# Gated delta rule: state steps that multiply keys by the state and send the residual through the inverse

## The reference, cut to what matters

```python
u = jnp.einsum('bhnij,bhnjv->bhniv', t_inv, v * beta)
w = jnp.einsum('bhnij,bhnjk->bhnik', t_inv, k_beta * jnp.exp(g)[..., None])
intra = jnp.einsum('bhnik,bhnjk->bhnij', q, k) * decay
q_dec = q * jnp.exp(g)[..., None]
k_dec = k * jnp.exp(g_last[..., None] - g)[..., None]

def step(state, inp):
    u_n, w_n, q_n, intra_n, k_n, dec_n = inp
    v_new = u_n - jnp.einsum('bhck,bhkv->bhcv', w_n, state)
    o_n = jnp.einsum('bhck,bhkv->bhcv', q_n, state) + jnp.einsum('bhcs,bhsv->bhcv', intra_n, v_new)
    state = state * dec_n[..., None, None] + jnp.einsum('bhck,bhcv->bhkv', k_n, v_new)
    return state, o_n
```

## Time and profile before

| what | value |
|---|---|
| runs | 1976.20, 1977.56, 1979.18 us |
| profiled execution, span | 1977.9 us |
| PE busy | 1908.4 us, 96% |
| DVE busy | 1473.9 us, 75% |
| ACT busy | 982.2 us, 50% |
| POOL busy | 314.5 us, 16% |
| mean DMA rate | 202 GB/s |
| chain that ended last | PE 70%, DVE 13%, DMA 6%, ACT 5%, issue 5% |
| eight heads | about 500 to 1134 us from the span's start |

### The profile page before, as it was taken

The page is one execution under the profiler, slowest core; times in us unless marked ns, Lnnn a source line. Parts: engine busy times, 40 slices in busy tenths (PEclk is TensorE's granted clock), DMA queues, the critical chain, the costliest instruction groups (busy, mean ns, idle before and its releaser), DMA issues.

```text
span 1977.9 us, 28478 instructions
## 1 busy us (share of the span) xinstructions
PE 1908.4 (96%) x9519; PEld 1584.6 (80%) x9519; DVE 1473.9 (75%) x1966; ACT 982.2 (50%) x1354; POOL 314.5 (16%) x243
## 2 busy tenths in 40 slices
PE   5999999999999999999999899998999999999996
PEld 5778888778888888888888787876888888888883
DVE  6966676676756858658577455677999999999996
ACT  5343223301453544535535343125888788788863
POOL 0332323001102101021011000001222222222210
PEclk7999999999999999999999999998999999999998
DMA  8133223687132222222232678437999999999966
GB/s 301 32 82 103 68 80 106 213 294 248 40 106 72 70 75 77 80 70 71 84 93 59 206 266 262 140 143 280 372 383 383 382 380 381 386 387 383 400 252 257
DMA packets 225500, 398.93 MB, mean 202 GB/s; under 512 B 50805, under 2 KB 163878, under 8 KB 199974
## 3 DMA queue, kind: packets, MB, share of 16 engines
q1 hardware_dynamic: 205254, 342.28, 49.8%
q10 hardware_dynamic: 10976, 39.15, 5.1%
q0 software_dynamic: 9216, 16.80, 2.2%
HBM read 356.89 MB, written 58.06 MB: 210 GB/s over the span
## 4 chain that ended last, share of the span: by engine, by line
PE 70%; DVE 13%; DMA 6%; ACT 5%; issue 5%; SPq 1%; ACTq 0%; DVEq 0%; POOL 0%; POOLq 0%
PE ps L3152 17%; PE ps L2756 13%; PE ps L769 12%; PE ps L3196 9%; PE ps L3047 4%; PE ps L2786 3%; PE ps L3138 1%; DVE vv L2019 1%; DMA inv_rows<-inv_d 1%; DMA so_lo<-o_lo_d 1%; DMA inv_d<-sub_x 1%; PE ps L2950 1%; PE ps L2980 1%; PE ps L3176 1%; PE ps L2994 1%
## 5 line engine op out<-in xcount | busy, mean ns | idle before, releaser
L637 DVE TENSOR_TENSOR mw_lo<-mw_raw,mw_hi 128x2048 fp32r<-128x2048 f32 x192 | 436.9, 2290 | 44.0 <-ACT mw_hi L632 43.8
L632 ACT ACTIVATE mw_hi<-mw_raw 128x2048 fp32r<-128x2048 f32 x192 | 368.1, 1919 | 116.2 <-PE ps L3152 67.0
L769 PE MATMUL ps<-h_hi,w_lo 128*128 128x512 f32 x704 | 287.9, 409 | 3.0 <-ACT mod_rows L1447 1.3
L769 PE MATMUL ps<-h_hi,w_hi 128*128 128x512 f32 x704 | 275.5, 391 | 0.0
L769 PE MATMUL ps<-h_lo,w_hi 128*128 128x512 f32 x704 | 274.9, 391 | 0.0
L3152 PE MATMUL ps<-mw_hi,xT_lo 128*128 128x512 f32 x512 | 203.9, 398 | 3.1 <-DVE xT_lo L2525 2.3
L3152 PE MATMUL ps<-mw_hi,xT_hi 128*128 128x512 f32 x512 | 201.1, 393 | 0.0
L3152 PE MATMUL ps<-mw_lo,xT_hi 128*128 128x512 f32 x512 | 200.3, 391 | 0.0
L769 PEld LDWEIGHTS ps<-h_hi,w_hi 128*128 128x128 f32 x704 | 132.6, 188 | 28.4
L769 PEld LDWEIGHTS ps<-h_hi,w_lo 128*128 128x128 f32 x704 | 133.0, 189 | 26.6 <-ACT conv_in L1454 1.8
L769 PEld LDWEIGHTS ps<-h_lo,w_hi 128*128 128x128 f32 x704 | 133.2, 189 | 22.3
(11 more groups left out here) (436 smaller groups left out, 4042.4 us busy)
## 6 DMA issues: line engine op xcount, KB each, us to landing
mw_raw<-in_w_dram SPq DMA_DIRECT2D x192, 1024.0 KB, 8.2
w_raw<-in_w_in_dram SPq DMA_DIRECT2D x44, 512.0 KB, 5.0
ada_h<-in_w_ada_dram SPq DMA_DIRECT2D x32, 512.0 KB, 6.0
pair_w<-in_w_in_dram SPq DMA_DIRECT2D x28, 512.0 KB, 4.8
y_t<-y_d SPq DMA_DIRECT2D x7, 1024.0 KB, 10.1
ada_sc<-in_w_ada_dram SPq DMA_DIRECT2D x4, 1024.0 KB, 8.7
s_d<-sc_acc ACTq DMA_DIRECT2D x8, 512.0 KB, 5.5
gate_b_d<-gate_sig ACTq DMA_DIRECT2D x8, 512.0 KB, 5.0
```

What stands on the lines that cost most here:

```text
L632: act.activation(mw_hi[off % NSPLIT][:], mw_raw[off % NRAW][:], ACT.Copy).then_inc(mw_hi_done, 1)
L637: dve.tensor_tensor(mw_lo[off % NSPLIT][:], mw_raw[off % NRAW][:], mw_hi[off % NSPLIT][:], ALU.subtract).then_inc(mw_lo_done, 1)
L769: last = pe.matmul(dst, lhs[:, s, k], rhs[:, k, cols], start=(k == 0 and part == 0), stop=(k == KD - 1 and part == 2))
```

## The change

The product of `k_bg` with `Y` and its copy `w_neg` are gone, and so are the `k_bg` copies. (The squares that used `k_bg` as a place to write go to a tile `square_out`.) The scale of the keys, now with the sign turned, is applied by a new DVE instruction in each step from t = 1: it multiplies the product of keys and state by the scale and adds it to `v_beta` in place (`r_done`). Only then does PE multiply `Y` by `v_beta`. So a step has three places where PE waits (`s_ready`, `r_done`, `vn_done`) and not two, and the six projection products of a step are dealt out two to each. On DVE the convolution's tap moves ahead of the state update.

```diff
@@ the projection helper
-                for part in range(3):
+                for part in parts:
@@ ACT, start of a head
-                act.wait_ge(k_root, 6 * h + 6)
-                act.wait_ge(k_dec_done, TT * h + TT)
-                for t in range(TT):
-                    act.activation(k_bg[:, t], ..., ACT.Copy, scale=hk[:, K_BG, t:t + 1]).then_inc(k_bg_done, 1)
@@ ACT, ahead of the state loop
-                for n in range(2):
-                    act.wait_ge(w_mm, past(2 * h + n + 1))
-                    act.activation(w_neg[:, 4 * n:4 * n + 4]..., ps[:, 6 + n], ACT.Copy,
-                                   scale=-1.0).then_inc(w_neg_done, 1)
@@ DVE, the state loop
+                dve.wait_ge(v_beta_done, TT * h + TT)
                 for t in range(TT):
+                    if t > 0:
+                        dve.wait_ge(ks_mm, (TT - 1) * h + t)
+                        dve.scalar_tensor_tensor(out=v_beta[:, t], in0=ps[:, 6 + t % 2, 0:P],
+                                                 scalar=hk[:, K_BG, t:t + 1], in1=v_beta[:, t],
+                                                 op0=ALU.mult, op1=ALU.add).then_inc(r_done, 1)
+                    if t >= 4 and not last:
+                        if t == 4:
+                            dve.wait_ge(bank_free, 2 + 2 * head_tile(h, 3) + 1)
+                        conv_tap(h + 1, 1, 1, qk[:, 1], 0, k_conv, t - 4)
                     if t < TT - 1:
                         dve.wait_ge(ds_mm, (TT - 1) * h + t + 1)
...
-                    if t >= 4 and not last:
-                        if t == 4:
-                            dve.wait_ge(bank_free, 2 + 2 * head_tile(h, 3) + 1)
-                        conv_tap(h + 1, 1, 1, qk[:, 1], 0, k_conv, t - 4)
@@ PE
-                for a in range(2):
-                    pe.wait_ge(y_upd, 2 * NL * h + 2 * (NL - 1) + a + 1)
-                    for t in range(4 * a, 4 * a + 4):
-                        last_mm = pe.matmul(ps[:, 6 + a, ...], k_bg[:, t], Y[:, t], start=True, stop=True)
-                    last_mm.then_inc(w_mm, 1)
...
                 for t in range(TT):
-                    if t % 4 == 0:
-                        pe.wait_ge(w_neg_done, 2 * h + t // 4 + 1)
+                    if t == 0:
+                        pe.wait_ge(y_upd, 2 * NL * h + 2 * NL)
+                    tok = slice(t * P, (t + 1) * P)
                     o_t = ps[:, 3 + t % 2, 0:P]
-                    last_mm = pe.matmul(ps[:, 2, 0:P], Y[:, t], v_beta[:, t], start=True, stop=(t == 0))
                     if t > 0:
                         pe.wait_ge(s_ready, (TT - 1) * h + t)
-                        last_mm = pe.matmul(ps[:, 2, 0:P], w_neg[:, t], S[:], start=False, stop=True)
-                    last_mm.then_inc(vn_mm, 1)
-                    if t >= 2:
-                        pe.wait_ge(o_copied, past(TT * h + t - 1))
-                    if t > 0:
+                        pe.matmul(ps[:, 6 + t % 2, 0:P], qk[:, 1, tok], S[:], start=True, stop=True).then_inc(ks_mm, 1)
+                        if t >= 2:
+                            pe.wait_ge(o_copied, past(TT * h + t - 1))
                         pe.matmul(o_t, S[:], q_dec[:, t], start=True, stop=False)
-                    filler(2 * t)
+                        filler(6 * t, 6 * t + 2)
+                        pe.wait_ge(r_done, (TT - 1) * h + t)
+                    pe.matmul(ps[:, 2, 0:P], Y[:, t], v_beta[:, t], start=True, stop=True).then_inc(vn_mm, 1)
+                    filler(6 * t + 2 if t else 0, 6 * t + 4)
                     pe.wait_ge(vn_done, TT * h + t + 1)
                     if t < TT - 1:
                         pe.matmul(ps[:, 5, 0:P], k_dec[:, t], v_new[:, t % 2], start=True, stop=True)\
                           .then_inc(ds_mm, 1)
                     pe.matmul(o_t, v_new[:, t % 2], intra[:, t], start=(t == 0), stop=True).then_inc(o_mm, 1)
-                    filler(2 * t + 1)
+                    filler(6 * t + 4, 6 * t + 6)
```

More of the change, by code:

```diff
@@ L260, in decoder_block @@
     intra = at("intra", [P, TT, P])
-    k_bg = at("k_bg", [P, TT, P])
+    square_out = at("square_out", [P, TT, P])
     k_dec = at("k_dec", [P, TT, P])
@@ L295, in decoder_block @@
     assert top[0] <= SCRATCH + 2 * 4 * TT * P
-    top[0] = SCRATCH + 4 * TT * P
-    w_neg = at("w_neg", [P, TT, P])
+    top[0] = SCRATCH + 2 * 4 * TT * P
     o_raw = at("o_raw", [P, T])
@@ L510, in decoder_block @@
         vt_mm = sem("vt_mm")
-        k_bg_done = sem("k_bg_done")
         k_dec_done = sem("k_dec_done")
@@ L521, in decoder_block @@
         y_upd = sem("y_upd")
-        w_mm = sem("w_mm")
-        w_neg_done = sem("w_neg_done")
+        ks_mm = sem("ks_mm")
+        r_done = sem("r_done")
         s_ready = sem("s_ready")
@@ L603, in decoder_block @@
                  q_dec_done, head_out, logits_done, h_hi_done, h_lo_done, mb_out, o_copied, x1_turned,
-                 sc_copied, gb_sig, root_done, x1T_done, w_mm, *m_out, *h2_out]
+                 sc_copied, gb_sig, root_done, x1T_done, *m_out, *h2_out]
         SHIFT_PARTS = KD + 1
@@ L1475, in key_norms @@
                         act.wait_ge(kt_mm, 2 * h + t // 4 + 1)
-                    ins = act.activation(k_bg[:, t], ps[:, 4 + t // 4, (t % 4) * P:(t % 4 + 1) * P], ACT.Square,
+                    ins = act.activation(square_out[:, t], ps[:, 4 + t // 4, (t % 4) * P:(t % 4 + 1) * P], ACT.Square,
                                          accum_out=k_stat[:, 0, t:t + 1])
@@ L1523, in head_act @@
                 evac_conv("head", h, 0, 0, 1)
-                act.wait_ge(k_root, 6 * h + 6)
-                act.wait_ge(k_dec_done, TT * h + TT)
-                for t in range(TT):
-                    act.activation(k_bg[:, t], ps[:, 4 + t // 4, (t % 4) * P:(t % 4 + 1) * P], ACT.Copy,
-                                   scale=hk[:, K_BG, t:t + 1]).then_inc(k_bg_done, 1)
                 evac_conv("head", h, 0, 1, 1)
@@ L1550, in head_act @@
                                    scale=hk[:, K_V, t:t + 1]).then_inc(v_beta_done, 1)
-                for n in range(2):
-                    act.wait_ge(w_mm, past(2 * h + n + 1))
-                    act.activation(w_neg[:, 4 * n:4 * n + 4].rearrange("p t i -> p (t i)"), ps[:, 6 + n], ACT.Copy,
-                                   scale=-1.0).then_inc(w_neg_done, 1)
                 for t in range(TT):
@@ L1950, in _ @@
             dve.wait_ge(gate_exp, 5)
-            dve.tensor_tensor(gates[:, G_KBG], grow_of[:].rearrange("p h t -> p t h"), gates[:, G_BETA], ALU.mult).then_inc(gate_step, 1)
+            dve.tensor_tensor(gates[:, G_KBG], grow_of[:].rearrange("p h t -> p t h"), gates[:, G_NBETA], ALU.mult).then_inc(gate_step, 1)
             dve.wait_ge(gate_step, 9)
@@ L2933, in head_pe @@
                             pe.wait_ge(kk_done, 4 * h + 4)
-                            pe.wait_ge(k_bg_done, TT * h + TT)
                             pe.wait_ge(k_dec_done, TT * h + TT)
@@ L2945, in head_pe @@
                             last_mm.then_inc(yl_mm, 1)
-                for a in range(2):
-                    pe.wait_ge(y_upd, 2 * NL * h + 2 * (NL - 1) + a + 1)
-                    for t in range(4 * a, 4 * a + 4):
-                        last_mm = pe.matmul(ps[:, 6 + a, (t % 4) * P:(t % 4 + 1) * P], k_bg[:, t], Y[:, t],
-                                            start=True, stop=True)
-                    last_mm.then_inc(w_mm, 1)
                 pe.wait_ge(q_dec_done, past(h + 1))
@@ L2958, in head_pe, with filler @@
                     bank_clear(pe, head_tile(H - 1, 3), 1)
[L2960 to L2974, removed]
+                def filler(first, end):
+                    width = H - 1 if last else KD
+                    for n in range(first, min(end, 2 * 3 * width)):
+                        half, k, part = n // (3 * width), n // 3 % width, n % 3
+                        if last and half == 0 and part == 0:
+                            pe.wait_ge(o_in[k // 4], (128, 96)[k // 4])
+                        if not last and k == 0 and part == 0:
+                            wait_w(pe, "head", h, 3)
+                            bank_clear(pe, head_tile(h, 3), half)
+                        phase, hi, lo = ("merge", so_hi, so_lo) if last else ("head", h_hi, h_lo)
+                        last_mm = project(pe, ps[:, half], phase, 0 if last else 3, hi, lo, half, ks=(k,), parts=(part,))
+                        if not last and k == KD - 1 and part == 2:
+                            last_mm.then_inc(proj_done, 1)
```

## The result

The changed kernel takes 1991.18 us (median of five runs, 1987.90 to 1992.79), the kernel before 1977.56 us (median of five) beside it. The medians differ by 13.6 us; the ratio is 1.0065, 95% interval 1.0053 to 1.0076, which is 12.9 us (10.5 to 15.0). Forecast were 1993.9 us and +16.3. The profiled execution has a span of 1989.2 us, 11.3 above that of before.

What follows compares the result with a forecast made beforehand. The heads' state loop was taken as bound by PE's own stream plus uncovered waits. Terms -8.0 + 11.6 + 10.6 + 2.1 = +16.3 us on the 1977.6 us median gave 1993.9 us; range 1985.5 to 2002.

Steps and rivals of the forecast that it cites:

- The bound: State loop of the heads: bound by PE's own stream; a wait costs only what projection products ahead do not cover.
- Start of the loop: Heads 0 to 6, before step 0: w_neg's products and wait go, v_beta late next; gain 1.14 us a head, 8.0 for seven.
- Steps: Heads 0 to 6, each loop step: three partly uncovered waits, 2.50 to 2.74 us; 1.65 us a head, 11.6 for seven.
- The restart of 0.16 us: PE at a wait nothing covers: load 0.05 us after the operand, product counted as started 0.11 us behind its load.
- The tap: DVE at step 4, heads 0 to 6: state update waits behind tap and conv_in copy; 1.52 us a head, 10.6 for seven.
- The last head: Last head: start gain swallowed by waits for DMA-fed fillers; later waits and uncovered step 7 add 2.1 us together.
- At nothing: Removed k_bg copies on ACT, seven more DVE instructions a head, step 7's output nearer the loop's end: no cost counted.
- The sum: Whole kernel: -8.0 + 11.6 + 10.6 + 2.1 = +16.3 us, giving 1993.9 us; chance 0.78.
- The hidden restart: Rival at the step waits: they cost only the lower bound; +6.7 us, 1984.3 us; chance 0.05.
- the covered tap: Rival at step 4: ACT copies conv_in ahead of DVE's wait, so 10.6 us go; +5.7, 1983.3 us; chance 0.03.
- the covered chain: Rival in the heads: DVE passes step 4's wait without a stop; -3.4 us, 1974.2 us, or 1972.1; chance 0.03.
- this rival: Clock rival in the heads: stalls lower PE's granted clock; 2008 us if in every head, 2000 if in some; chance 0.08.

Runs made afterwards that it cites:

- the products back: Changed kernel plus eight unused products of k_dec and Y and two ScalarE copies before the loop: heads 0 to 6 1998.35 us; last head only 1992.05 us.
- the run with seven products: Changed kernel with seven projection products in a step instead of six, in heads 0 to 6: 1993.88 us, ratio 1.0080.
- the tap first: Kernel before with only the convolution's tap moved ahead of the state update on DVE: 1985.71 us, ratio 1.0032.

## Why the prediction was right, step by step

- **The bound.** PE's stream and what it waits for in the loops made the heads 1.70 us longer; 2.03 were forecast (-1.14 + 1.65 + 1.52). The direction and each mechanism came as forecast; the sum, +16.3, was 2.7 us above the medians' 13.6. The sizes below explain 1.9 of that (14.4 us measured at the end of the heads).
- **Start of the loop.** Forecast -1.14, with v_beta late next; measured -1.12, released by v_beta. With the products back, the start is later again.
- **Steps.** Forecast 2.74 us, measured 2.72, with all three waits and v_new's the longest. A head paid 1.70 + 1.12 - 1.42 = 1.40 us for its steps where 1.65 was forecast, 1.8 us over seven heads. The restart of 0.16 us, paid three times a step, is the term that was slightly dear: behind the two DVE waits the product starts 0.14 to 0.15 us after the operand's end (640.29 to 640.43, 638.50 to 638.65). What I had not seen as such: with two products ahead of each wait the round trips 0.93 + 0.93 + 0.86 = 2.72 close to a ring longer than PE's 2.50. By this sum no other way of dealing out six products could mend it; no other dealing was run. The seventh product, which made the step 0.05 us longer and not 0.23, speaks for the ring.
- **The tap.** Forecast 1.52, measured 1.42; nearly all of the difference is the state update's start 0.09 us before the tap's end. Shown from both sides, by moving it in either kernel.
- **The last head.** Forecast: the gain at its start is swallowed, 2.1 us are added behind the second DMA. Measured: swallowed, 2.0 us. The second landing itself came 0.4 us later in the head (14.17 us behind the last level's first product, 13.75 before), which the forecast had put at nothing. So the last head costs 2.4 us, and that this offsets a part of what the steps were overpriced is luck.
- **At nothing.** Right for ACT's copies and DVE's new instructions, and for step 7's output, which comes a product nearer to the loop's end: the rest of the head is 1.32 us shorter, and the start's 1.12 and that product's 0.23 account for it. I took PE's work outside the loops for free of any other bound; the run with seven products shows it had about 0.4 us to spare. It did not decide here.
- **The sum.** At step 7 of the last head the profiled executions differ by 14.4 us (1132.99, 1147.36); seven heads give 11.9 and the last one 2.4 (forecast 14.2 and 2.1). At the end they differ by 11.3, by the medians 13.6. In the stages behind the heads the profile after has shorter waits (for one DMA of gathered rows 2.3 in place of 3.5 us), but single runs of one kernel spread over 5 us, so how much of the 3 us comes back by the change stays open.
- **Rivals.** The hidden restart falls with the loads that stand 0.05 us behind their release; the covered tap and the covered chain fall with the 1.60 us at step 5. The clock stayed at 1.00 in all seven loops. The Trainium skill, page "TensorE: Matmul & The Clock Gate", section "HAM oscillation — how this bites in real kernels", has as its case waits for DMA that are longer than these stalls. The prediction left that out when it gave its rule to this rival, so the 1.00 here does not test that case. The clock fell in one place that I had not named, the last head (below).

## What to carry to other kernels

When a loop carries a value through several engines, add up its round trips (reaction, instruction, restart) and hold the sum against the busiest engine's work in a pass. The step was not below the larger of the two in any run here (2.72 us at 2.72 and 2.50; 2.77 at 2.72 and 2.73), and an algebra that saves products but adds a round trip pays the difference in every step. When an instruction of another stream is moved ahead of one on the ring, ask what it waits for, not how long it is: the tap is 0.5 us and cost 1.4. And before removing work from the bound engine, look for the chain beside it that is nearly as long.

## What the runs showed of the hardware

PE's granted clock in the last head of the kernel after (length, busy, PEclk, DMA share, GB/s):

```profile
1124.00:1126.00 2.00, 1.31 (x3) 0.50 1.02 412
1126.00:1128.00 2.00, 2.00 (x8) 0.50 1.02 410
...
1130.00:1132.00 2.00, 2.00 (x14) 1.00 1.08 342
```

It fell to 0.50 (1.2 of 2.4 GHz) in the second of two idle times close together, 1.71 us for Y and 3.10 for the DMA. The other six runs without the products in the last head show the same (1.71 and 2.54 to 3.56 us idle, then 0.50). With the eight products put back between them (idle 1.28 and 1.40) it was 1.00 throughout, also over the 2.01 us at the second DMA. But the products alone do not decide: the kernel before kept 1.00 over its 2.58 us at the second DMA, and with the tap first, its products in place, the clock fell to 0.50 over 2.45 us at the same point. What decides between these two stays open.

The fall after the change cost nothing: PE ran slowly up to the second DMA, for which it then waited 0.16 us, and 2.01 us with the products back. From the first landing to step 7's output both took the same, 22.67 us (1124.69 to 1147.36) and 22.66 (1124.15 to 1146.81).

Two DVE instructions that do not depend on each other can overlap by about 0.1 us in the records: the state update from PSUM began 0.09 us before the tap ended (644.08 against 644.17). In the kernel before, a tap began 0.09 us before the state update's end (643.86 against 643.95).
